# Splitting each weight item into high and low parts in two halves instead of at once

## The reference, cut to what matters

```python
x = x + hybrid_mixer(rms_norm(x, norm_mix[l]), w_in[l], ...)
x = x + memory_cross_attention(rms_norm(x, norm_cross[l]), mem_n, w_cq[l], w_ckv[l], w_co[l])
x = x + conv_ffn(rms_norm(x, norm_ffn[l]), w_up[l], conv_w[l], conv_b[l], w_down[l])
...
proj = h @ w_in
x = x + (g_a * (o_a @ w_pa) + g_b * (o_b @ w_pb)) @ w_o
return x + jnp.square(jax.nn.relu(h @ w_up)) @ w_down
```

## Time and profile before

| | |
|---|---|
| median of 3 runs | 3277.18 us (3276.04 to 3277.9) |
| the profiled execution's own time | 3276.37 us |
| its span, first to last instruction | 3274.5 us |
| TensorE busy | 3015.2 us, 92% |
| VectorE busy | 1598.2 us, 49% |
| ScalarE busy | 1312.9 us, 40% |
| DMA queue of SyncE | 487.73 MB, 41.6% of 16 engines |
| mean granted clock of TensorE | 0.948 |

### The profile page before, as it was taken

The page is one execution under the profiler, slowest core; times in us unless marked ns, Lnnn a source line. Parts: engine busy times, 40 slices in busy tenths (PEclk is TensorE's granted clock), DMA queues, the critical chain, the costliest instruction groups (busy, mean ns, idle before and its releaser), DMA issues.

```text
span 3274.5 us, 35733 instructions
## 1 busy us (share of the span) xinstructions
PE 3015.2 (92%) x13916; PEld 2472.5 (76%) x13916; DVE 1598.2 (49%) x1668; ACT 1312.9 (40%) x1442; POOL 50.7 (2%) x94
## 2 busy tenths in 40 slices
PE   8998764998999999989899997898899999999998
PEld 6876554876887778877777876788787887888786
DVE  4433335455555445545545656544565444444443
ACT  4323332355444334434444446323334443334433
POOL 1001000000000000000010000000000000000000
PEclk9988775998999999999999999898999999999999
DMA  7533120543554555545465433222545555555453
GB/s 271 194 121 106 52 85 7 212 164 116 183 187 147 183 195 186 178 141 182 159 240 197 147 123 135 84 94 81 204 170 179 186 185 193 191 181 186 179 187 129
DMA packets 78222, 518.95 MB, mean 158 GB/s; under 512 B 9561, under 2 KB 9777, under 8 KB 23713
## 3 DMA queue, kind: packets, MB, share of 16 engines
q1 hardware_dynamic: 71616, 487.73, 41.6%
q0 software_dynamic: 6496, 29.70, 2.5%
HBM read 508.98 MB, written 12.35 MB: 159 GB/s over the span
## 4 chain that ended last, share of the span: by engine, by line
PE 86%; DVE 6%; ACT 4%; issue 1%; DVEq 1%; DMA 0%; ACTq 0%; SPq 0%; POOL 0%; POOLq 0%
PE acc L294 25%; PE acc L296 25%; PE acc L295 24%; DVE w_lo L202 2%; ACT w_hi L197 2%; PE wk L818 1%; PE wk L787 1%; PE wk L1457 1%; PE wk L1362 1%; PE wk L2124 1%; PE wk L801 1%; PE wk L2122 1%; PE wk L790 1%; PE wk L2115 1%; ACT h_hi L482 0%
## 5 line engine op out<-in xcount | busy, mean ns | idle before, releaser
L202 DVE TENSOR_TENSOR w_lo<-w_raw,w_hi 128x2048 fp32r<-128x2048 f32 (+1 forms) x484 | 1059.8, 2190 | 1153.5 <-ACT w_hi L197 1145.7
L197 ACT ACTIVATE w_hi<-w_raw 128x2048 fp32r<-128x2048 f32 (+1 forms) x484 | 887.7, 1834 | 1139.1 <-PE acc L296 1111.7
L294 PE MATMUL acc<-w_hi,h_hi 128*128 128x512 f32 (+1 forms) x2528 | 1013.4, 401 | 64.7 <-DVE w_lo L202 19.3
L295 PE MATMUL acc<-w_lo,h_hi 128*128 128x512 f32 (+1 forms) x2528 | 997.1, 394 | 0.0
L296 PE MATMUL acc<-w_hi,h_lo 128*128 128x512 f32 (+1 forms) x2528 | 996.7, 394 | 0.0
L294 PEld LDWEIGHTS acc<-w_hi,h_hi 128*128 128x128 f32 x2528 | 486.4, 192 | 182.3 <-issue 55.0
L296 PEld LDWEIGHTS acc<-w_hi,h_lo 128*128 128x128 f32 x2528 | 484.7, 192 | 102.4
L295 PEld LDWEIGHTS acc<-w_lo,h_hi 128*128 128x128 f32 x2528 | 485.8, 192 | 97.2
L294 PE MATMUL acc<-w_hi,f_hi 128*128 128x512 f32 x856 | 342.3, 400 | 15.4 <-DVE x L344 7.5
L296 PE MATMUL acc<-w_hi,f_lo 128*128 128x512 f32 x856 | 338.4, 395 | 0.0
L295 PE MATMUL acc<-w_lo,f_hi 128*128 128x512 f32 x856 | 337.4, 394 | 0.0
(11 more groups left out here) (382 smaller groups left out, 2182.3 us busy)
## 6 DMA issues: line engine op xcount, KB each, us to landing
w_raw<-in_w_up_a SPq DMA_DIRECT2D x76, 1024.0 KB, 4.8
w_raw<-in_w_up_b SPq DMA_DIRECT2D x72, 1024.0 KB, 4.8
w_raw<-in_w_win SPq DMA_DIRECT2D x52, 1024.0 KB, 4.8
w_raw<-in_w_merge SPq DMA_DIRECT2D x32, 1024.0 KB, 4.8
w_raw<-in_w_down_a SPq DMA_DIRECT2D x32, 1024.0 KB, 4.8
w_raw<-in_w_down_b SPq DMA_DIRECT2D x32, 1024.0 KB, 4.8
w_raw<-in_w_win2g SPq DMA_DIRECT2D x24, 1024.0 KB, 4.9
w_raw<-in_w_down_a SPq DMA_DIRECT2D x24, 768.0 KB, 4.2
```

Of the source, the lines that this page charges most:

```text
L197: act_.activation(w_hi[:, s % SPL, 0:k], w_raw[:, s % RAW, 0:k], ACT.Copy).then_inc(hi_ready, 1)
L202: dve_.tensor_tensor(w_lo[:, s % SPL, 0:k], w_raw[:, s % RAW, 0:k], w_hi[:, s % SPL, 0:k].bitcast(F32), ALU.subtract).then_inc(lo_ready, 1)
L294: pe_.matmul(o, xh, wh, start=kt == 0, stop=False)
L295: pe_.matmul(o, xh, wl, start=False, stop=False)
```

## The change

ScalarE and VectorE split each item in two instructions, over the first half of the k-tiles (rounded up) and the rest. Each of them raises `hi_ready` or `lo_ready` by one, so both now count two per item, and every wait for them is rewritten with twice the number. VectorE waits for each half of `w_hi` by itself. TensorE waits for the first half of `w_lo` at the item's start, and on the first token tile again before the first k-tile of the second half. SyncE's loads still wait for the whole of the item four before.

```diff
                         if not (first and self.b + j < RAW):
-                            e.wait_ge(lo_ready, i - RAW + 1)
+                            e.wait_ge(lo_ready, (i - RAW + 1) * 2)
...
+            def parts(self, j):
+
+                m = -(-self.kts[j] // 2) * self.width
+                return [(0, m), (m, self.cols(j))]
+
             def make_hi(self, e, n, j):
-                i, s, k = self.b + n * self.ipc + j, self.slot(n, j), self.cols(j)
+                i, s = self.b + n * self.ipc + j, self.slot(n, j)
                 e.wait_ge(raw_ready[s % RAW], self.count(n, j) * 16)
                 if not (isinstance(n, int) and i < SPL):
                     e.wait_ge(item_done, i - SPL + 1)
-                act_.activation(w_hi[:, s % SPL, 0:k], w_raw[:, s % RAW, 0:k], ACT.Copy).then_inc(hi_ready, 1)
+                for a, b in self.parts(j):
+                    act_.activation(w_hi[:, s % SPL, a:b], w_raw[:, s % RAW, a:b], ACT.Copy).then_inc(hi_ready, 1)
 
             def make_lo(self, e, n, j):
-                i, s, k = self.b + n * self.ipc + j, self.slot(n, j), self.cols(j)
-                e.wait_ge(hi_ready, i + 1)
-                dve_.tensor_tensor(w_lo[:, s % SPL, 0:k], w_raw[:, s % RAW, 0:k],
-                                   w_hi[:, s % SPL, 0:k].bitcast(F32), ALU.subtract).then_inc(lo_ready, 1)
+                i, s = self.b + n * self.ipc + j, self.slot(n, j)
+                for p, (a, b) in enumerate(self.parts(j)):
+                    e.wait_ge(hi_ready, i * 2 + p + 1)
+                    dve_.tensor_tensor(w_lo[:, s % SPL, a:b], w_raw[:, s % RAW, a:b],
+                                       w_hi[:, s % SPL, a:b].bitcast(F32), ALU.subtract).then_inc(lo_ready, 1)
...
-                e.wait_ge(lo_ready, self.b + n * self.ipc + j + 1)
+                i = self.b + n * self.ipc + j
+                e.wait_ge(lo_ready, i * 2 + 1)
...
                     for k in range(self.kts[j]):
+                        if t == self.tiles[0] and k == -(-self.kts[j] // 2):
+                            e.wait_ge(lo_ready, i * 2 + 2)
                         kt = sum(self.kts[:j]) + k
```

## The result

The kernel with halves took 3247.19 us (median of 4 runs, 3243.6 to 3249.09), the kernel before, measured with it, 3277.54 (3276.04 to 3279.18): a ratio of 0.9905, with a 95% interval from 0.989 to 0.9921. That is 30.4 us less, where 21.5 were forecast. The same changed kernel measured again, with the experiments, took 3249.93 (ratio 0.9911, 0.9896 to 0.9926), so the gain is 28 to 30 us by the two medians. The profiled execution took 3248.42 us, its span was 3246.6.

A forecast was written before the change was run, and what follows sets the result against it. The prediction took TensorE, 86% of the chain of waits, as the bound, with time to win only where it stands still or could start sooner. 17.5 + 5.0 - 1 = 21.5 us off 3277.2 gave 3255.5 us, range 3241 to 3267.

The forecast's parts named there:

- Waits for w_lo: TensorE's matmuls wait for w_lo 31.4 us in 18 waits; halves were to save 17.5 us.
- Evacuations behind make_lo: At chunks' first items VectorE evacuates after making w_lo; ending the split sooner was to save 5.0 us in all.
- boundary of the earlier trace: At a chunk boundary near 1083 us, TensorE's wait for the evacuation was to fall from 1.2 to 0.9 us.
- Added work: 484 more instructions on each of ScalarE (some 97 us) and VectorE (77 us) were to cost 1 us net.
- The wait in mid-item: TensorE's one more wait in each item was to cost 0.
- What would vanish: TensorE's waits for w_lo at 660 to 800, 1690 to 1726 and after 2540 us were to vanish.
- the sentence on SyncE's loads: SyncE's loads are released with the second half, 0.7 us sooner; no load is awaited, so the effect was nothing.
- the term of 4.1 us: At 1690 to 1726 us, items of 256-wide matmuls: four waits removed, less VectorE's lateness, 4.1 us saved.
- 1952 to 2019: Three waits for w_lo, 5.9 us, with VectorE busy with a convolution: 2.0 us to be saved.
- The first: Rival: the wait in mid-item costs TensorE 0.09 us an item, 46 us in all, giving 3302 us; chance 0.07.
- The second: Rival: TensorE starts earlier but waits later, only every third microsecond survives, giving 3271 us; chance 0.10.
- The third: Rival: five low clock stretches behind shortened waits vanish, 7 us more gain, giving 3248 us; chance 0.15.

The follow-up runs named there:

- half the bytes: The kernel with halves, loading only the first half of the columns of the items of the two cmp stages: 3245.16 us (ratio 0.9901).
- high parts in one instruction: The kernel with halves, but ScalarE makes an item's w_hi in one instruction again; VectorE and TensorE keep their halves: 3269.05 us (ratio 0.9967).
- four parts: Against the kernel with halves, items split into four parts of 512 columns, three or two for items of three or two k-tiles: 3238.39 us (ratio 0.988).

## Why the prediction was right, and where it was off

**The forecast held**: faster, inside the range (3241 to 3267), by the mechanism it named. Against its own list:

- *Waits for w_lo, 17.5 us.* 31.4 fell to 11.9: 19.5.
- *Evacuations behind make_lo, 5.0 us.* Line 344 gave 2.9, line 2381 1.6, line 330 0.7, the barrier 0.8 (2.90 us to 2.10, at 1181 us): 6.0. At the boundary of the earlier trace rows the wait was to be 0.9; it was 0.82:

```profile
1072.34 0.50 PE L304 MATMUL acc<-w_hi,f_hi 128*128 128x512 f32 x1 [0.82 <-DVE x L354]
```

- *Added work, -1.* DVE's busy time rose by 32 us and ACT's by 48, not by 77 and 97. Two instructions back to back on one engine overlap: a pair takes 2.36 us on VectorE and 2.01 on ScalarE, where two alone would take 2.44 and 2.12. None of it is seen on the path, so this term was 0. The Trainium skill ("VectorE: DVE Perf Modes", section on the TRN2 errata) has a fixed latency paid per instruction; the single durations bear that out, and the busy time says that a part of it is hidden when the next instruction needs nothing new.
- *The wait in mid-item, 0.* Shown twice: 228.6 us for 40 items before and after, and no more with eight waits an item.
- *Two slips.* At 1690 to 1726 us, 5.2 - 1.0 is 4.2 and not 4.1, and 3277.2 - 21.5 is 3255.7 and not 3255.5. Neither matters.
- *What would vanish.* The waits of 660 to 800 us and after 2540 are gone. Those of 1690 to 1726 are not: three of 0.2 to 0.4 us are left.

**The step that failed** inside this sum is the sentence on SyncE's loads: "no load is awaited, so nothing". It held for the kernel before. With TensorE's waits gone, ScalarE waited 7.8 us in 4 waits for the last loads of the 256-wide stages and the one behind, and the term of 4.1 us gave 2.0 of idle time and, less 0.9 of clock, 1.1 in all. The barrier wait at the end of the first of the two stages grew by 0.6 us, as forecast (0.5); the one at the end of the second grew from 0.6 to 2.5. With half the bytes it was 1.2, and the stretch had 4.6 us back. The time of that stretch had been set by the split; the next limit, at a DMA share of 0.92 before, was close behind it, and stood in the same row of the windows view that I had read for other columns.

**The terms that were too small.** The idle time fell by 22.8 us, against 21.5 forecast, with errors of both signs inside, so that the two lie so close is in part luck. The forecast had 2.1 too much at the loads and 0.5 too much at 1952 to 2019. It had 1.0 too little for added work, 1.0 at the evacuations (0.36 instead of 0.25 at each of six boundaries is most of it), and 1.1 between 1730 and 1952 us, a stretch that I had costed at nothing because no wait for w_lo shows in it. There line 894's waits for lp fell from 3.6 us to 2.6; that a split that ended sooner let VectorE start this work sooner is likely, but not shown. From 758 to 1032 us the idle time fell by 0.8, which is the third forecast wait, at 799 us; the other 1.7 us of the gain are clock, whose low stretch of 743 to 763 us (20.4 us) lasted 13.7 in all. What lies above 22.8 is not the mechanism: 3.2 us of clock and 1.9 of the last output's landing, in this one profile. The repeat shows 26.4 us up to the last matmul and none at the end, with 23.0 of idle time. So the mechanism is worth about 23 us here, and the rest of the medians' 27.7 and 30.4 is clock and scatter.

**The rivals.** The first is refuted by the run with more waits. The second came true in two places only: at 1952 to 2019 us 5.9 us of waits became 2.0 and 1.2 us reached the end, since the wait ahead of the next stage grew from 1.3 to 4.1; and at 1692 to 1730 the barrier's wait took a part. The third said that up to 7 us more would come as low stretches of the clock vanish. The clock gave 3.2 us in the first trace and 4.5 in the repeat, but most of it before 1032 us, away from the waits that it meant, and at the wait it named first the contrary happened. TensorE's wait at 1042 us is 1 us shorter than before, and behind it:

```profile
1041.50:1044.50 3.00, 2.63 (x6) 2.15 (x7) 2.65 (x4) 1.05 (x2) 0.00 (x0) 0.50 0.31 86
1045.00:1048.00 3.00, 3.00 (x8) 2.31 (x7) 0.00 (x0) 0.00 (x0) 0.00 (x0) 0.50 0.72 275
```

It ran at 0.50 (1.2 GHz) for 6.8 us, twice the stretch of the earlier trace rows; between 1032 and 1183 us it was idle 2.8 us less and busy 1.2 us more. So a shorter wait doesn't by itself buy clock. By the Trainium skill ("TensorE: Matmul & The Clock Gate", section on the HAM clock gate) the clock follows recent activity; these rows neither confirm nor refute that, but they forbid my use of it, that less idle time must mean more clock.

**Still open.** It stays unexplained why the stretch from 2019 to 2346 us takes 327.4 to 327.8 us in five traces (before, with halves twice, high parts in one instruction, more waits) and 329.5 to 329.8 in the six others, with the same 38.7 us idle each time. Its matmuls arrive at other moments, and the clock is low for 58 to 61 us of it or for 65. Which moment decides was not tried. Nor do the runs show exactly what TensorE's early start is worth: 8 to 11 us by the medians, 5.9 by idle time, with clock and scatter between them.

## What to carry to other kernels

Cut a two-engine chain of preparation in two, and the second engine works beside the first: that alone gave about two thirds of the gain here, even for a consumer that waits for the whole. Make the parts so that each arrives before the consumer has used up the one before; equal parts of the consumer's step did this, a short part ahead of a long one didn't. And where a stage's waits go, look up at once what share the DMA engines had there: in the one stage here where it was 0.92, the loads were the next bound.

## What the hardware showed beside that

- Waits that are already met cost TensorE nothing that shows: up to 8 an item instead of 2 changed 228.6 us to 228.7 for some 40 items.
- Two instructions of a split whose inputs are ready overlap by 0.08 us (VectorE, 1024 columns: 2.36 us for two of 1.22) and 0.1 us (ScalarE: 2.01 for two of 1.06). With four parts the mean on VectorE was 684 ns.
- Weight loads of 1024 KB, one every 3.8 us beside GpSimd's transfers, filled the DMA engines: share 0.99 at 380 GB/s.
- Most of the granted clock's low stretches came at the same moments, within 0.6 us, in two traces of one kernel; one at 44 us was in the second only, and one that ended at 2034 us lasted 10.2 us instead of 6.8. In traces of edited kernels more of them moved. That is 1 to 3 us in stages that an edit doesn't touch. An edit worth 2 us of idle time can't be judged by the total.
